# Causal attention inside a two-block kernel: one VectorE pass for mask, maximum and scaling, normalising on POOL, copies of the turned weights in turns

## The chip, the cores and the metric

The kernel runs on one core of a Trainium2 chip. The metric is the device time of one execution in microseconds. Before the change the median of three runs is 2840.65 us (2839.79 to 2842.64).

## What is computed

Two transformer blocks run one after the other over 1024 tokens of width 1024. The second block mixes tokens with an mLSTM and with multi-head attention, and the change lies in the attention. It has 8 heads. A query or key has 96 features (64 plain, 32 rotated), a value 64.

```python
def causal_block_attention(q, k, v):
    scale = dq ** -0.5
    def one_block(args):                     # 128 queries against all keys
        qblk, bi = args
        sc = jnp.einsum('bhqd,bkhd->bhqk', qblk, kf) * scale
        sc = jnp.where(kpos[None, :] <= qpos[:, None], sc, -jnp.inf)
        p = jax.nn.softmax(sc, axis=-1)
        return jnp.einsum('bhqk,bkhd->bqhd', p, vf)
```

In the kernel the mLSTM follows the attention, and behind both comes the output projection with the weights `w_out_2`.

## The kernel before

The five engines run programs of their own, written out by hand, and meet at counting semaphores (`wait_ge`). Within an engine the order is that of the code. The attention is in `mla_pe`, `mla_dve`, `mla_act`, `mla_pool` and `mla_sp` (PE is TensorE, DVE is VectorE, ACT is ScalarE, POOL is GpSimd, SP issues loads).

The work is cut into 64 blocks, listed in `NQ` (L2185). A block is one head and 128 queries. The two heads of a pair alternate, and the block of queries grows from i = 0 to 7, so the rows of block n have N = 128 (i + 1) keys: two blocks of 128, two of 256, up to two of 1024, and this four times. Keys beyond the block of queries are not computed.

For each block n TensorE computes the scores into the PSUM tile `PS[n % 2]` (`scores`, L2367). VectorE adds the triangular mask `negm` to the last 128 columns in place (L2319), takes the maximum of each row (L2321) and multiplies it by minus the scale (L2323). ScalarE computes the exponentials from PSUM into the SBUF tile `x4[:, n % 2]`, and their sum (L2243). VectorE inverts the sum (L2310) and multiplies the row by it (`normalise`, L2312). TensorE transposes the row in pieces of 128x128 into `PS[2]` (`turn`, L2377). ScalarE copies it to one of four tiles `turned_p` in SBUF (`pt_copy`, L2268). For each pair of blocks TensorE multiplies the turned weights with the values into `PS[3]` (`values`, L2390), and every fourth pair a half row of results leaves (`mixa` on ScalarE L2278, `mixa_low` on VectorE L2283).

The orders: TensorE takes scores(n + 2), turn(n), and after each odd n the values of the pair before. VectorE takes mask, maximum and scaling of block n, then normalises block n - 1. ScalarE takes the exponentials of block n, then the copy of block n - 1. The scores of n + 2 wait until the exponentials of n are done. A turn waits until the copy of the block before it is done. In the last sixteen blocks ScalarE and VectorE also do first steps of the mLSTM between blocks (`head_hi` L2454, `head_lo` L2464, `mask_dve` L2540, `log_weight_act` L2546).

POOL splits fp32 weights into a high and a low part by two passes over tensors (L499, L503, `split_unit`; for the heads' weights L483, L485). During the attention it waits for the sixteenth result (`pv_ready`), and then splits two units of `w_out_2`, in pieces of 256 columns. `in2_pool` (L1936 on) is its part of the projection before the attention, with one small memset (L1944).

## Time and profile before

| | us |
|---|---|
| median of 3 runs | 2840.65 |
| the profiled execution | 2838.5 |
| its span | 2836.8 |
| TensorE busy | 2729.4 (96%) |
| VectorE busy | 1814.4 (64%) |
| POOL busy | 1277.9 (45%) |
| ScalarE busy | 1021.3 (36%) |

The profile is of one execution on the chip, and the attention lies between 1780 and 1953 us of its span. A line names the engine, the line of the kernel (L2312), the operation, and output and inputs as `out<-in`. Idle before is the time for which the engine stood still before an instruction, with what ended it. PEld is the loading of TensorE's stationary operand, which overlaps its products (PE). The granted clock is a share of TensorE's full speed.

### The profile page before, as it was taken

To read this page: it belongs to the slowest core of one execution; us is meant where nothing else is said; L and a number is where in the kernel's file an instruction comes from. 1 tells how busy PE (TensorE), PEld (TensorE's weight loads), DVE (VectorE), ACT (ScalarE), POOL (GpSimd) and SP (SyncE) were. 2 spreads that over 40 slices of the span, in tenths; PEclk is the share of its full clock that TensorE was granted. 3 is DMA by queue.
4 is the path that set the end of the run, shared out by engine and by line. 5 is a ranking of instruction groups with operands and counts; after the bars stand their busy time and mean duration, and the time that the engine had idled before them with its cause. 6 is when DMAs were issued, how large, how long until landed. Compare 5 with 4: busy or idle time off the path is not lost.

```text
span 2836.8 us, 32978 instructions
## 1 busy us (share of the span) xinstructions
PE 2729.4 (96%) x12578; PEld 2155.0 (76%) x12578; DVE 1814.4 (64%) x2070; ACT 1021.3 (36%) x1397; POOL 1277.9 (45%) x780
## 2 busy tenths in 40 slices
PE   7999999999999999999998999889998999999998
PEld 5888788787777888887786887555587788878777
DVE  3111355655747766669879758776637766777887
ACT  4000323332214333334444014665535433344444
POOL 2433322223436988884333444102332888833321
PEclk9999999999999999999999999999899999999999
DMA  5223232324442333336631534103333345565543
GB/s 180 96 95 108 88 119 90 119 90 156 148 141 79 100 112 102 90 118 215 205 115 49 187 112 117 33 33 97 102 127 104 119 141 163 173 206 163 163 134 134
DMA packets 336967, 348.90 MB, mean 123 GB/s; under 512 B 18915, under 2 KB 256602, under 8 KB 336822
## 3 DMA queue, kind: packets, MB, share of 16 engines
q1 hardware_dynamic: 327254, 311.30, 35.6%
q10 hardware_dynamic: 9568, 35.66, 3.2%
q8 instruction: 93, 1.52, 0.2%
q14 instruction: 52, 0.43, 0.0%
HBM read 237.53 MB, written 108.34 MB: 122 GB/s over the span
## 4 chain that ended last, share of the span: by engine, by line
PE 51%; DVE 10%; issue 2%; ACT 2%; DMA 1%; POOL 1%; SPq 0%; DVEq 0%; ACTq 0%; POOLq 0%
PE ps L3282 34%; PE ps L533 9%; DVE op_lo L3359 2%; PE ps L2367 1%; PE ps L2740 1%; DVE sw_lo L3192 1%; PE ps L2390 1%; DVE small L2321 1%; PE ps L2377 1%; DVE x L2312 1%; PE ps L2858 1%; DVE acc L3603 1%; DVE acc L3610 0%; PE ps L2713 0%; DVE acc L1889 0%
## 5 line engine op out<-in xcount | busy, mean ns | idle before, releaser
L3282 PE MATMUL ps<-op_hi,sw_hi 128*128 128x512 f32 x1769 | 692.6, 392 | 15.5 <-DVE op_lo L3359 8.2
L3282 PE MATMUL ps<-op_hi,sw_lo 128*128 128x512 f32 x1769 | 689.1, 390 | 0.0
L3282 PE MATMUL ps<-op_lo,sw_hi 128*128 128x512 f32 x1769 | 688.9, 389 | 0.0
L499 POOL TENSOR_TENSOR w_hi_t<-w_raw,ones 128x1024 fp32r<-128x1024 f32 (+1 forms) x85 | 162.1, 1910 | 735.7 <-PE ps L533 354.7
L3282 PEld LDWEIGHTS ps<-op_hi,sw_hi 128*128 128x128 f32 x1769 | 332.4, 188 | 96.8 <-issue 16.8
L3282 PEld LDWEIGHTS ps<-op_hi,sw_lo 128*128 128x128 f32 x1769 | 332.4, 188 | 69.2
L3282 PEld LDWEIGHTS ps<-op_lo,sw_hi 128*128 128x128 f32 x1769 | 332.6, 188 | 68.7 <-issue 0.5
L656 DVE TENSOR_TENSOR stage<-ps,rstd 128x1024 f32<-128x1024 f32 x62 | 75.8, 1222 | 345.4 <-PE ps L533 326.9
L3182 ACT ACTIVATE sw_hi<-sw_sumNone 128x512 fp32r<-128x512 f32 (+1 forms) x252 | 157.1, 624 | 330.3 <-PE ps L3282 247.0
L533 PE MATMUL ps<-h1hi,w_hi_t 128*128 128x512 f32 x720 | 233.5, 405 | 13.0 <-DVE h1lo L617 9.0
L3192 POOL TENSOR_TENSOR sw_lo<-sw_sumNone,sw_hi 128x512 fp32r<-128x512 f32 x138 | 214.7, 1565 | 33.2 <-ACT sw_hi L3182 33.1
L533 PE MATMUL ps<-h1lo,w_hi_t 128*128 128x512 f32 x720 | 227.4, 397 | 0.0
L533 PE MATMUL ps<-h1hi,w_lo_t 128*128 128x512 f32 x720 | 227.0, 396 | 0.0
L503 POOL TENSOR_TENSOR w_lo_t<-w_raw,w_hi_t 128x1024 fp32r<-128x1024 f32 (+1 forms) x85 | 217.6, 2563 | 6.2
L3143 POOL TENSOR_TENSOR sw_sumNone<-sw_raw 128x512 f32<-128x512 f32 (+1 forms) x63 | 113.4, 1800 | 232.4 <-DVE sw_lo L3192 209.5
L3182 ACT ACTIVATE sw_hi<-sw_raw 128x512 fp32r<-128x512 f32 (+1 forms) x189 | 117.4, 622 | 200.6 <-PE ps L3282 198.8
L3192 POOL TENSOR_TENSOR sw_lo<-sw_raw,sw_hi 128x512 fp32r<-128x512 f32 x109 | 159.7, 1466 | 53.7 <-ACT sw_hi L3182 53.7
L533 PEld LDWEIGHTS ps<-h1hi,w_hi_t 128*128 128x128 f32 x720 | 133.8, 189 | 52.3 <-issue 10.5
L533 PEld LDWEIGHTS ps<-h1lo,w_hi_t 128*128 128x128 f32 x720 | 135.8, 189 | 33.4
L533 PEld LDWEIGHTS ps<-h1hi,w_lo_t 128*128 128x128 f32 x720 | 135.8, 189 | 33.2
L3158 POOL TENSOR_TENSOR sw_sumNone<-sw_raw,sw_sumNone 128x512 f32<-128x512 f32 (+1 forms) x63 | 91.4, 1450 | 87.5 <-DVE sw_lo L3192 84.8
L3150 POOL TENSOR_TENSOR sw_sumNone<-sw_sumNone,sw_raw 128x512 f32<-128x512 f32 (+1 forms) x63 | 98.7, 1566 | 61.6 <-DVE sw_lo L3192 58.9
(444 smaller groups left out, 4877.2 us busy)
## 6 DMA issues: line engine op xcount, KB each, us to landing
op_raw<-hidden SPq DMA_DIRECT2D x42, 1024.0 KB, 8.6
w_raw<-in_w_in SPq DMA_DIRECT2D x60, 512.0 KB, 3.9
sw_raw<-in_w_ffn_in SPq DMA_DIRECT2D x44, 512.0 KB, 5.3
proj<-stage ACTq DMA_DIRECT2D x42, 512.0 KB, 2.6
hidden<-hidden_blocks SPq DMA_DIRECT2D x13, 1536.0 KB, 6.2
acc<-proj SPq DMA_DIRECT2D x36, 512.0 KB, 4.5
hidden<-hidden_blocks SPq DMA_DIRECT2D x14, 1280.0 KB, 5.0
sw_raw<-in_w_up SPq DMA_DIRECT2D x32, 512.0 KB, 8.3
```

Of the source, the lines that this page charges most:

```text
L499: ins = pool.tensor_tensor(whi[:, u.par, s], raw[:, u.par, s], ones[:, 0:1].to_broadcast([P, n]), ALU.mult)
L503: ins = pool.tensor_tensor(wlo[:, u.par, s], raw[:, u.par, s], whi[:, u.par, s].bitcast(F32), ALU.subtract)
L533: mm = pe.matmul(out[:, b * HALF:(b + 1) * HALF], w, x[:, k, b * HALF:(b + 1) * HALF], start=(begin and k == ks[0] and n == 0), stop=(end ...
L656: dve.tensor_tensor(stage[:, u.par, :], PS[u.par if pair is None else pair][:, :], rstd[:, :], ALU.mult).then_inc(S["unit_out"][u.par], 1)
L2312: dve.tensor_scalar(x4[:, n % 2, 0:N], x4[:, n % 2, 0:N], sm(n, 3), None, ALU.mult)\
L3143: pool.tensor_tensor(s1, a21, a22, ALU.add).then_inc(S["sw_sum"], 1)
L3150: pool.tensor_tensor(s2, s1, a11, ALU.subtract).then_inc(S["sw_sum"], 1)
L3158: pool.tensor_tensor(s2, a12, s2, ALU.subtract).then_inc(S["sw_sum"], 1)
L3182: act.activation(wshi[ring(m)][:, 0:n], weight_block(p, r), ACT.Copy).then_inc(S["sw_hi"], 1)
L3192: eng.tensor_tensor(wslo[ring(m)][:, 0:n], weight_block(p, r), wshi[ring(m)][:, 0:n].bitcast(F32), ALU.subtract).then_inc(S["sw_lo"], 1)
L3282: mm = pe.matmul(out, w, x[:, k, :], start=(k == 0 and i == 0 and r < 4), stop=(k == n - 1 and i == 2), skip_group_check=r >= 4)
L3359: dve.tensor_tensor(lo_of(first, r)[:, :, :], fresh_of(first, r)[:, :, :], hi_of(first, r)[:, :, :].bitcast(F32), ALU.subtract).then_inc(S ...
```

## The change

Constants: while the projection before the attention runs, POOL also makes `mask_row`, a row of 1024 columns that is zero but for the triangle in its last 128.

VectorE: mask, maximum and scaling become one instruction, `tensor_tensor_reduce`. It adds the scores (PSUM) and the end of `mask_row` (SBUF), multiplies by minus the scale, writes the row to `x4[:, n % 4]`, and writes each row's minimum. ScalarE's exponentials read this row, with scale -1, and write it in place. Four rows of `x4` are in use instead of two, and the turned weights get four tiles of their own. The scores of n + 2 wait for the fused pass of n instead of its exponentials.

POOL: it multiplies each row by its inverse sum (64 `tensor_scalar` with one scalar for each partition), and after each odd block from 17 to 47 it does one piece of 256 columns of the two splits of `w_out_2`, which no longer wait for `pv_ready`.

Copies of the turned weights: ScalarE does those of the odd blocks up to 61, VectorE those of the even blocks and the last. VectorE's order is now: fused pass of block n, reciprocal of block n - 1, and for even n the copy of block n - 2.

The places where the mLSTM's first steps (`turn_v`, `weight_scores`) waited for the exponentials now wait for the fused pass.

```diff
@@ -1942,6 +1943,11 @@
                 if j == 2:
                     pool.wait_ge(S["unit_done"], U_IN2 + 2)
                     pool.memset(cb[:, :, 0:3], 0.0).then_inc(S["ml_consts"], 1)
+                    pool.memset(mask_row[:, :], 0.0).then_inc(S["ml_consts"], 1)
+                    pool.wait_ge(S["ml_consts"], 2)
+                    last = mask_row[:, T - P:T]
+                    pool.affine_select(out=last, in_=last, compare_op=ALU.is_ge, fill=-BIG, base=0,
+                                       pattern=[[-1, P]], channel_multiplier=1).then_inc(S["ml_consts"], 1)
...
-        turned_p = [x4[:, 2, :], x4[:, 3, :]] + [at(f"p_turned{n}", [P, T], kb)[:, :] for n, kb in ((2, 107.5), (3, 111.5))]
+        turned_p = [at(f"p_turned{n}", [P, T], kb)[:, :] for n, kb in enumerate((75.03125, 107.5, 79.03125, 111.5))]
...
@@ -2205,7 +2211,28 @@
             for h in range(8):
                 for i in range(2):
                     split_head(pool, h, i)
-            pool.wait_ge(S["pv_ready"], 16)
+            for n, (h, i) in enumerate(NQ):
+                N = (i + 1) * P
+                pool.wait_ge(S["rs_inv"], n + 1)
+                pool.tensor_scalar(x4[:, n % 4, 0:N], x4[:, n % 4, 0:N], sm(n, 2), None, ALU.mult)\
+                    .then_inc(S["p_norm"], 1)
+                if 16 <= n < 48 and n % 2:
+                    wo2_piece(pool, (n - 16) // 2)
+
+        def wo2_piece(pool, p):
+            u, i = Step(U_WO2 + p // 8), p % 8
+            s = slice(i % 4 * 2 * P, i % 4 * 2 * P + 2 * P)
+            if i == 0:
+                pool.wait_ge(S["w_landed"][u.par], u.landed())
+                pool.wait_ge(S["unit_done"], u.times(1, -1))
+            if i == 4:
+                pool.wait_ge(S["w_hi"], u.times(1, 1))
+            if i < 4:
+                ins = pool.tensor_tensor(whi[:, u.par, s], raw[:, u.par, s], ones[:, 0:1].to_broadcast([P, 2 * P]), ALU.mult)
+            else:
+                ins = pool.tensor_tensor(wlo[:, u.par, s], raw[:, u.par, s], whi[:, u.par, s].bitcast(F32), ALU.subtract)
+            if i % 4 == 3:
+                ins.then_inc(S[("w_hi", "w_split")[i // 4]], 1)
...
-                act.wait_ge(S["s_stat"], 2 * n + 2)
-                if n >= 2:
-                    act.wait_ge(S["pt_ready"], n - 1)
-                act.activation(x4[:, n % 2, 0:N], PS[n % 2][:, 0:N], ACT.Exp, bias=sm(n, 1), scale=QK_SCALE,
-                               accum_out=sm(n, 2)).then_inc(S["p_ready"], 1)
-                if n:
+                act.wait_ge(S["s_stat"], n + 1)
+                act.activation(x4[:, n % 4, 0:N], x4[:, n % 4, 0:N], ACT.Exp, bias=sm(n, 0), scale=-1.0,
+                               accum_out=sm(n, 1)).then_inc(S["p_ready"], 1)
+                if n and n % 2 == 0:
                     pt_copy(act, n - 1)
                 if n % 16 == 11:
...
         def sm(n, what):
 
-            c = 40 + 5 * (n % 2) + what
+            c = 40 + 3 * (n % 4) + what
             return small[:, c:c + 1]
...
+        def pt_copy_dve(dve, n):
+
+            N = (NQ[n][1] + 1) * P
+            dve.wait_ge(S["pt_ready"], n + 1)
+            if n >= 4:
+                dve.wait_ge(S["pv_ready"], n - 3)
+            dve.tensor_copy(turned_p[n % 4][:, 0:N], PS[2][:, 0:N]).then_inc(S["pt_out"], 1)
...
@@ -2303,26 +2334,22 @@
...
-            def normalise(n):
-
-                N = (NQ[n][1] + 1) * P
-                dve.wait_ge(S["p_ready"], n + 1)
-                dve.reciprocal(sm(n, 3), sm(n, 2)).then_inc(S["rs_inv"], 1)
-                dve.wait_ge(S["rs_inv"], n + 1)
-                dve.tensor_scalar(x4[:, n % 2, 0:N], x4[:, n % 2, 0:N], sm(n, 3), None, ALU.mult)\
-                   .then_inc(S["p_norm"], 1)
-
+            dve.wait_ge(S["ml_consts"], 3)
+            dve.wait_ge(S["q_rope"], 8)
             for n, (h, i) in enumerate(NQ):
                 N = (i + 1) * P
                 dve.wait_ge(S["s_ready"], n + 1)
-                late = PS[n % 2][:, N - P:N]
-                dve.tensor_tensor(late, late, negm[:, :], ALU.add).then_inc(S["s_masked"], 1)
-                dve.wait_ge(*count("s_masked", n + 1))
-                dve.tensor_reduce(sm(n, 0), PS[n % 2][:, 0:N], AX.X, ALU.max).then_inc(S["s_stat"], 1)
-                dve.wait_ge(S["s_stat"], 2 * n + 1)
-                dve.tensor_scalar(sm(n, 1), sm(n, 0), -QK_SCALE, None, ALU.mult).then_inc(S["s_stat"], 1)
+                if n == 3:
+                    dve.wait_ge(S["vh_t"], 8)
+                if n >= 4:
+                    dve.wait_ge(S["pt_ready"], n - 3)
+                dve.tensor_tensor_reduce(x4[:, n % 4, 0:N], PS[n % 2][:, 0:N], mask_row[:, T - N:T], -QK_SCALE, BIG,
+                                         ALU.add, ALU.min, sm(n, 0)).then_inc(S["s_stat"], 1)
                 if n:
-                    normalise(n - 1)
+                    dve.wait_ge(S["p_ready"], n)
+                    dve.reciprocal(sm(n - 1, 2), sm(n - 1, 1)).then_inc(S["rs_inv"], 1)
+                if n >= 2 and n % 2 == 0:
+                    pt_copy_dve(dve, n - 2)
                 if n % 16 == 12:
...
-            normalise(63)
+            dve.wait_ge(S["p_ready"], 64)
+            dve.reciprocal(sm(63, 2), sm(63, 1)).then_inc(S["rs_inv"], 1)
+            pt_copy_dve(dve, 62)
+            pt_copy_dve(dve, 63)
...
@@ -2361,7 +2391,7 @@
...
                 if n >= 2:
-                    pe.wait_ge(S["p_ready"], n - 1)
+                    pe.wait_ge(S["s_stat"], n - 1)
...
-                    tr = pe.transpose(PS[2][:, j * P:(j + 1) * P], x4[:, n % 2, j * P:(j + 1) * P], ident[:, :])
+                    tr = pe.transpose(PS[2][:, j * P:(j + 1) * P], x4[:, n % 4, j * P:(j + 1) * P], ident[:, :])
...
@@ -3882,8 +3912,6 @@
             f1_pool(pool)
             in2_pool(pool)
             mla_pool(pool)
-            for j in range(2):
-                split_unit(pool, Step(U_WO2 + j), pieces=4)
             mlstm_pool(pool)
```

## Rows read from the trace of the kernel before

**Rows 1.** Busy time by stretch: engines with instruction counts, granted clock, DMA share, GB/s

```profile
1780.00:1953.00 173.00, 150.69 (x1070) 96.28 (x1070) 126.05 (x338) 106.73 (x214) 10.57 (x16) 0.97 0.06 20
```

**Rows 2.** Waits before turns, by quarter; us in total, times, longest

```profile
PE ps L2377 <- DVE x L2312: 1.5, 4, 0.5
...
PE ps L2377 <- DVE x L2312: 3.9, 7, 0.9
PE ps L2377 <- ACT p_turned L2268: 2.0, 2, 1.0
...
PE ps L2377 <- DVE x L2312: 3.3, 7, 0.9
PE ps L2377 <- ACT p_turned L2268: 1.0, 1, 1.0
...
PE ps L2377 <- DVE x L2312: 6.8, 8, 1.4
```

**Rows 3.** Timeline, second and third quarter: start us, us, what, idle before

```profile
1840.03 0.49 DVE L2312 TENSOR_SCALAR x<-x,small 128x512 f32<-128x512 f32 x1
...
1879.00 0.30 DVE L2319 TENSOR_TENSOR ps<-ps,negm 128x128 f32<-128x128 f32 x1 [0.79 <-PE ps L2367]
...
1879.34 0.82 DVE L2321 TENSOR_REDUCE small<-ps 128x1 f32<-128x640 f32 x1
...
1880.27 0.15 DVE L2310 RECIPROCAL small<-small 128x1 f32<-128x1 f32 x1
...
1880.46 0.49 DVE L2312 TENSOR_SCALAR x<-x,small 128x512 f32<-128x512 f32 x1
...
1881.00 0.65 PE L2377 MATMUL ps<-ident,x 128*128 128x128 f32 x4 [0.51 <-DVE x L2312]
```

**Rows 4.** Groups of the attention stage by shape: count, busy us, mean ns, idle before

```profile
L2321 DVE TENSOR_REDUCE small<-ps 128x1 f32<-128x1024 f32 x8 | 9.8, 1225 | 0.3
L2312 DVE TENSOR_SCALAR x<-x,small 128x1024 f32<-128x1024 f32 x8 | 6.0, 754 | 0.3
L2312 DVE TENSOR_SCALAR x<-x,small 128x128 f32<-128x128 f32 x8 | 2.3, 288 | 0.3
L2243 ACT ACTIVATION_READ_ACCUMULATOR x<-ps,small 128x1 f32 x64 | 12.6, 197 | 0.0
L2268 ACT ACTIVATE p_turned<-ps 128x1024 f32<-128x1024 f32 x8 | 8.2, 1025 | 6.8 <-PE ps L2377 6.8
```

**Rows 5.** Groups of POOL by shape, whole span

```profile
L499 POOL TENSOR_TENSOR w_hi_t<-w_raw,ones 128x1024 fp32r<-128x1024 f32 x77 | 157.3, 2043 | 675.8 <-PE ps L533 354.7 <-DMA w_raw<-in_w_in 267.9 <-DMA w_raw<-in_w_branch_gla 30.1
L499 POOL TENSOR_TENSOR w_hi_t<-w_raw,ones 128x256 fp32r<-128x256 f32 x8 | 4.8, 624 | 59.9 <-PE ps L2390 59.9
L483 POOL TENSOR_TENSOR w_hi_t<-w_raw,ones 128x128 fp32r<-128x128 f32 x8 | 4.2, 524 | 10.3 <-PE ps L533 10.3
L860 POOL MEMSET wup<- 32x1024 f32 x1 | 0.9, 941 | 0.0
L681 POOL TENSOR_SCALAR_AFFINE_SELECT ident<-ident 128x128 f32<-128x128 f32 x1 | 0.3, 293 | 0.2 <-POOL negm L679 0.2
```

**Rows 6.** Timeline: VectorE beside POOL's splits, and POOL behind the small memset

```profile
1831.37 0.53 DVE L2312 TENSOR_SCALAR x<-x,small 128x256 f32<-128x256 f32 x1
...
1577.53 1.89 POOL L499 TENSOR_TENSOR w_hi_t<-w_raw,ones 128x1024 fp32r<-128x1024 f32 x1 [5.64 <-PE ps L533]
```

**Rows 7.** Instructions on the tile bytok, 1960 to 2060: ns min/median/max, starts

```profile
L2612 DVE RECIPROCAL bytok<-bytok x3: 203/203/203, 1977.4 to 2037.9; 128x8 f32<-128x8 f32 x3
...
L2618 DVE SCALAR_TENSOR_TENSOR bytok<-ps,bytok x3: 166/167/167, 1979.1 to 2039.6; 128x8 f32<-128x8 f32 x3
L2621 DVE TENSOR_SCALAR bytok<-bytok x3: 1984/1992/1992, 1979.3 to 2039.8; 128x8 f32<-128x8 f32 x3
```

**Rows 8.** One of four such instructions of line 2464 in the last quarter

```profile
L2464 DVE SCALAR_TENSOR_TENSOR q_parts<-stage,q_parts x1: 1223/1223/1223, 1913.8 to 1913.8; 64x1024 fp32r<-64x1024 f32 x1
```

**Rows 9.** Busy time by stretch, columns as in rows 1: start of the attention

```profile
1788.00:1792.00 4.00, 4.00 (x13) 1.75 (x12) 2.94 (x10) 2.11 (x6) 0.00 (x0) 0.50 0.00 0
```

More of the change, by code:

```diff
@@ L246 @@
          "out_row": ("kdt_ready", 8), "x3_squared": ("g_step", 24), "x3_summed": ("conv_step", 16), "qk_high": ("yb_ready", 8),
-         "qk_low": ("yb_scaled", 8), "s_masked": ("o_sum", 8),
+         "qk_low": ("yb_scaled", 8),
          "x3_last_spilled": ("mv_loaded", 64)}
@@ L437, in two_block_kernel @@
         orow = at("out_rows", [P, 4, T], R0 + 80)
+        mask_row = at("mask_row", [P, T], R0 + 128)
         ylast = at("y_last", [P, 2, HALF], R0 + 16)
@@ L2227, in mla_act @@
                 if h == 7:
-                    act.activation(small[:, 44:45], ones[:, 0:1], ACT.Exp)
+                    act.activation(small[:, 52:53], ones[:, 0:1], ACT.Exp)
                 act.wait_ge(S["unit_done"], uk.times(1, 1))
@@ L2254, in mla_act @@
                     log_weight_act(act, n - 58)
-            pt_copy(act, 63)
         def sm(n, what):
-            c = 40 + 5 * (n % 2) + what
+            c = 40 + 3 * (n % 4) + what
             return small[:, c:c + 1]
@@ L2679, in turn_v @@
             if h == 0:
-                pe.wait_ge(S["p_ready"], 64)
+                pe.wait_ge(S["s_stat"], 64)
             if h == 1:
@@ L2691, in weight_scores @@
             if n == 0:
-                pe.wait_ge(S["p_ready"], 63)
+                pe.wait_ge(S["s_stat"], 63)
             if J == 0:
```

## The prediction

> **What bounds the kernel now.** I read the busy time by stretches first. The change works in the attention stage, from 1780 to 1953 us, plus 1.2 us of constants earlier. There TensorE is busy for 150.7 of 173 us, VectorE for 126, ScalarE for 107 and POOL for 10.6 [rows 1]. So TensorE is close to its own load, and the change can gain no more than TensorE's idle time.
>
> Next, who made TensorE wait, by quarters of the stage (16 of the 64 blocks each; the same multiply of one quarter and of the next starts at 1840.03 and 1880.46, so a steady quarter takes 40.4 us [rows 3]). The turns (transposes) waited for VectorE's normalising for 1.5, 3.9, 3.3 and 6.8 us, and for ScalarE's copy of the turned weights for 2.0 (two waits, one of them at the end of the first quarter) and 1.0 us [rows 2]. That is 18.5 us in all: the cap of any gain, 0.65% of the run.
>
> Then the timeline of one pair of blocks, for the chain behind such a wait [rows 3]. TensorE's order is scores(n+2), turn(n), scores(n+3), turn(n+1), values. When the scores of block n+2 are complete (1879.00) VectorE, in order, adds the mask, reduces five blocks of 128 columns (0.82), scales, inverts the sum of block n+1 (1880.27), multiplies its four-block row (1880.46, 0.49), and only then can TensorE turn it, at 1881.00 after 0.51 idle. So it isn't VectorE's load that binds but its order: the row to be turned stands behind the whole pass over a later block. The second turn of each pair shows it. With k the width of the row in blocks of 128, those waits are 0.89, 0.77, 0.24, 0.51, 0.39, 0.27 and 0 for k = 1 to 7 (the first turn at k = 3 waits 0.25 more). At k = 8 the turn waits 1.0 for ScalarE's copy, which makes 4.3 us for that quarter [rows 2]. They add up to the 3.3 us and 7 waits of the third quarter's row; the 0.51 is shown in rows 3, and the others are its like.
>
> **The change, part by part.**
>
> *The mask and scaling go from VectorE.* Mask to reduction is 0.34 (1879.00 to 1879.34), the scaling about 0.08 between the end of the reduction and the reciprocal [rows 3]. The fused pass reads scores from PSUM and a mask row from SBUF, and writes a full row. I give it the reduction's duration, 1225 ns at 1024 columns [rows 4], which makes 0.16 + 0.133k. It must also deliver a minimum. The nearest row for such a read-out is ScalarE's, 197 ns [rows 4]. No VectorE instruction of the trace does this, so the cost is 0 to 0.19 on each chain, and could lie a little below 0 if the fused pass overlaps better. I take 0.05, nearer to the reduction, which delivers its result at no visible extra.
>
> *The multiply goes from VectorE to POOL.* VectorE took 288 ns at 128 columns and 754 at 1024 [rows 4], or 0.22 + 0.066k. In rows 3 the new order would be: fused pass 1879.00 to 1879.82, reciprocal to 1880.00, 0.05 to reach POOL, the multiply M(4), 0.05 to reach TensorE, so the turn starts at 1880.10 + M(4) instead of 1881.00. For any width the turn moves by M(k) - 0.64 - 0.066k. POOL has no such instruction in the trace. Above it is bounded by POOL's two-operand pass against a broadcast column, 524 ns at 128 and 2043 at 1024: about 0.33 + 0.2k. Below by an affine select, which reads one tensor (293 ns at 128), and by the pace of a memset (941 ns for 1024 columns): 0.18 + 0.107k [rows 5]. The operation reads one tensor, so I take it near the lower end, 0.22 + 0.12k: M(4) = 0.70, M(8) = 1.18. With this the turn moves by -0.42 + 0.054k: -0.37, -0.31, -0.26, -0.20, -0.15, -0.10 for k = 1 to 6, in sum -1.4 us for a quarter. At k = 7 there is no wait to win back.
>
> The Trainium skill (GPSIMD Engine Reference, § 4.1 Engine selection) says that POOL is about half as fast as VectorE on two-input elementwise work but roughly at line rate with one input. With its 1.03 cycles an element at 1.2 GHz (§ 3.1, Elementwise) M(4) would be about 0.44 plus a dispatch, an estimate from that page; the sum would then lie at my lower end. The trace shows the first half of this rule (524 to 2043 ns above) and nothing of the second.
>
> *Even copies of the turned weights go to VectorE.* turn(n+1) needs the copy of block n, and VectorE now starts it only after the fused pass of n+2 and the reciprocal of n+1. In rows 3 this is 1880.00 + 0.69 + 0.05 = 1880.74 against 1881.00, a gain of 0.26 at most at k = 4. Over the widths this path caps the gain at -0.45 + 0.066(k - 1). With my M it binds nowhere, with the lowest M from k = 3 on (a quarter then gains 1.7). At k = 8, where ScalarE's copy was what the turn waited for [rows 2], VectorE needs 1.22 instead of ScalarE's 1.02 for 1024 columns [rows 4]: +0.2 a quarter. VectorE's load over a pair falls even so (three passes over PSUM and two short ones instead of two masks, two reductions, two multiplies and four short ones), and ScalarE loses half of its copies. Its exponentials now read SBUF; I cost that at nothing, since they end well before VectorE comes to the reciprocal behind its next pass.
>
> *More buffers; TensorE's wait for scores(n+2) goes to the fused pass.* This wait hardly counted before, so nothing is gained.
>
> *Weight pieces on POOL.* The two units that POOL split in the second quarter (16 instructions, 10.6 us [rows 1]) now run as 16 pieces behind the odd multiplies of the second and third quarters. Before, they slowed VectorE's multiply: at 1831.37 it took 0.53 for 256 columns [rows 6], and the second quarter has 0.6 us more wait behind VectorE than the third [rows 2]. That goes. In its place a piece of some 0.62 us [rows 5] delays the next multiply where the row is narrow, some 0.3 a quarter. Net nothing. The next user of those weights is the projection behind the next stage.
>
> *POOL against VectorE on SBUF.* In the next stage, beside POOL, tiny VectorE instructions with a PSUM input or a reciprocal take 167 and 203 ns, but a scaling from SBUF to SBUF of the same 8 columns 1992 [rows 7]. The new VectorE work is of the two unhindered kinds. The Trainium skill (SBUF — State Buffer, § Who interferes with whom) says the same, and adds that VectorE instructions with two SBUF inputs block POOL's reads. Here these are four passes of 1.22 us for the next stage's heads in the last quarter [rows 8], each of which could hold one multiply back, up to 0.5 a time.
>
> *Last quarter.* Its 6.8 us of wait are 3.5 above the third quarter's, because those four passes (and four small ones) stand in VectorE's queue at narrow rows, where VectorE is full. The change takes about 1 us of VectorE's work from each such pair; I count 1.5 of the 3.5, between 0 and 3.
>
> *Constants.* A memset (0.94) and a select (0.29) [rows 5] stand on POOL's queue ahead of a weight split. POOL finished that one 5.64 us before TensorE let it begin the next [rows 6], so 1.3 us are hidden. Otherwise they would cost TensorE 1.3 once.
>
> **The sum**, against the profiled run's 2838.5 us (span 2836.8, 1.7 around it; the median of the timed runs is 2.15 above). Three quarters by -1.4 + 0.2 = -1.2, the first by -0.3 (it waits little, since TensorE runs at half clock there): -3.9. Last quarter's queue -1.5. Read-out 28 times 0.05: +1.4. Total -4.0: 2834.5 on the profiled run, 2836.7 as a median. Lower end: -1.5 three times, -0.5, -3.0 and -0.6 (no piece in the way): -8.6, so 2832. Upper end with POOL at its dear bound: below.
>
> **Rivals.**
>
> 1. *POOL's multiply becomes what the turns wait for: slower.* It takes over when M(4) passes about 0.84 (at 0.70 the gain is 4.0, and 28 turns a stage follow it one for one); slower by 0.2% from M(4) = 1.05. At the broadcast rate [rows 5] M(4) = 1.13: 28 x 0.43 = +12, and the first turn at k = 8 waits too (M(8) = 1.93), 0.9 in each quarter; less in the first, so about -4 + 14 = +10: 2851. With a dear read-out on top, 2856. For it: POOL is slow in every row where it computes, and its multiply sits on the path alone, with no neighbour to hide it. Against: all those rows stream two operands. Chance 0.22.
>
> 2. *The fused pass is dearer than a reduction.* With 0.19 more on each chain [rows 4] the sum is -4 + 28 x 0.14 = 0: 2840.6, the change of order does nothing. Chance 0.10.
>
> 3. *The clock.* After TensorE's idle at the stage's start its granted clock is 0.50 (1.2 GHz) in 1788 to 1792 [rows 9]. A stretch of 5 us at 0.50 costs 2.5 us of work. If the shifted pattern brings or saves one or two of them, the time moves by 2.5 to 5 either way: 2832 to 2842. Nothing in the change touches the idle that comes first, so I put 0.13.
>
> **How the numbers follow.** Forecast with its own range 2832 to 2840.6: 0.55. A measurement of this kernel tells 0.2% (5.7 us) from nothing: faster is below 2835.0, slower above 2846.3. The forecast gives 0.27 faster and 0.28 same; rival 1 0.19 slower and 0.03 same; rival 2 0.10 same; rival 3 0.05, 0.04 and 0.04. Together 0.32, 0.45 and 0.23. The range 2832 to 2852 leaves out rival 1 with a dear read-out and the lower tail, somewhat under 0.2.
>
> **What would show it.** Right: POOL's multiply near 0.70 us at 512 columns; TensorE's wait before turns about 13 to 15 us instead of 18.5, now put down to POOL and to VectorE's copy; the fused pass at 1.2 to 1.3 us for 1024 columns; a steady quarter of 39.2 instead of 40.4 us. Wrong: multiplies of over 1 us at 512 columns, a second instruction after each fused pass, VectorE's reciprocal or copy stretched beside POOL, or a difference that lies outside 1780 to 1953.

## The result and the profile after

The changed kernel takes 2861.22 us (median of 4 runs, 2858.78 to 2865.64) against 2840.86 us for the kernel before (2839.79 to 2842.64): the ratio is 1.0072, 95% interval [1.0057, 1.0087]. It is slower by 20.4 us, and lies above the forecast range.

The profiled execution of the changed kernel is the longest of the four (2865.64 us, span 2863.9), so its span is 27.1 us above that of before. Nearly 7 of that are not in the medians: this execution lies 4.4 above its median, and that of before 2.4 below its own. From the first score matmul of the attention to the first product on the tile Wt it takes 198.5 us (1777.6 to 1976.1), before 174.9 (1779.8 to 1954.7). All the attention figures below are read in this way. They are 23.6 us apart; the rest is small and scattered: 2.2 us less before the stage, 2.5 more in the next one, 3.2 more behind that.

First the busy time of the whole attention stage, the view of [rows 1], each kernel over its own stage. The line of after:

```profile
1778.00:1976.00 198.00, 155.94 (x1079) 99.95 (x1078) 88.15 (x243) 87.53 (x181) 122.64 (x81) 0.95 0.06 19
```

and the same view of the kernel before, over its 175 us (rows 1 stop 2 us earlier):

```profile
1780.00:1955.00 175.00, 152.69 (x1081) 97.49 (x1080) 126.15 (x339) 107.33 (x215) 11.80 (x17) 0.97 0.07 22
```

VectorE fell from 126 to 88 us and ScalarE from 107 to 88, as the change means. POOL rose from 12 to 123. TensorE's work is the same (1079 instructions against 1081); its idle time went from 22.3 to 42.1 us, and its busy time rose by 3.2 at a granted clock of 0.95 instead of 0.97. So 20 of the 23 us are waiting and 3 are longer busy time, which goes with the clock. Behind the start, the stage of before has a granted clock of 1.00 throughout. The changed kernel has two stretches there at 0.50, or 1.2 GHz (the first row takes in its edges). Each goes with one of TensorE's two longest waits for POOL: the clock fell just behind the wait of 2.13 us that ended at 1825.45, and during that of 2.19 us that ended at 1932.95. First the turn behind the earlier wait, then the busy time of both stretches, columns as in [rows 1]:

```profile
1825.45 1.54 PE L2407 MATMUL ps<-ident,x 128*128 128x128 f32 x8 [2.13 <-POOL x L2217]
...
1825.60:1829.10 3.50, 3.50 (x28) 3.17 (x29) 0.00 (x0) 1.40 (x3) 0.37 (x1) 0.55 0.00 0
1932.00:1938.60 6.60, 5.65 (x18) 3.22 (x19) 2.18 (x9) 3.18 (x7) 3.67 (x3) 0.50 0.00 1
```

TensorE is busy for 9.15 us in them; at full clock the same work would take about 4.4 us less (3.50 by 0.45, 5.65 by 0.50).

The waits of that stage (engine, line waited for, us in total, times, longest), which answer to [rows 2]:

```profile
DVE x L2346 <- PE ps L2397: 92.3, 39, 5.9
POOL x L2217 <- DVE small L2350: 79.8, 37, 14.8
PEld ps L2407 <- POOL x L2217: 62.6, 44, 3.0
...
PE ps L2407 <- POOL x L2217: 39.7, 34, 2.2
```

Line 2407 is the turn, 2217 POOL's multiply, 2346 the fused pass, 2350 the reciprocal. TensorE waited for POOL 39.7 us; before, its waits ahead of turns were 18.5 us [rows 2]. VectorE, whose idle time before was 49 us (175 less 126), now waits 92.3 us for scores. POOL itself waits 79.8 us for the reciprocal, so it isn't loaded to the brim: it is late.

The groups by shape say why. They answer to [rows 4] and [rows 5] (count, busy us, mean ns, idle before):

```profile
L2217 POOL TENSOR_SCALAR x<-x,small 128x1024 f32<-128x1024 f32 x8 | 22.7, 2843 | 1.2 <-DVE small L2350 0.6 <-DVE small L2362 0.6
...
L2217 POOL TENSOR_SCALAR x<-x,small 128x512 f32<-128x512 f32 x8 | 12.5, 1562 | 9.3 <-DVE small L2350 9.3
...
L2350 DVE RECIPROCAL small<-small 128x1 f32<-128x1 f32 x63 | 10.0, 158 | 0.5 <-ACT x L2268 0.3
L2346 DVE CUSTOM_DVE_ANT_0 x<-ps,mask_row 128x1024 f32<-128x1024 f32 x8 | 9.8, 1225 | 16.3 <-PE ps L2397 16.3
...
L2299 DVE COPY p_turned<-ps 128x1024 f32<-128x1024 f32 x5 | 6.1, 1224 | 6.3 <-PE ps L2407 6.3
...
L2346 DVE DVE_READ_ACCUMULATOR2_ANT small<- 128x1 f32 x64 | 5.3, 83 | 0.0
...
L2217 POOL TENSOR_SCALAR x<-x,small 128x128 f32<-128x128 f32 x8 | 4.8, 602 | 25.5 <-DVE small L2350 25.5
```

POOL's multiply of one tensor takes 602 ns at 128 columns, 1562 at 512 and 2843 at 1024: 0.28 + 0.32k with k in blocks of 128. I had given it 0.22 + 0.12k. The fused pass has the reduction's 1225 ns, and VectorE's copy 1224.

Last the timeline of a pair of blocks in the third quarter, which answers to [rows 3] (start us, us, what, idle before):

```profile
1894.86 0.96 DVE L2346 CUSTOM_DVE_ANT_0 x<-ps,mask_row 128x768 f32<-128x768 f32 x1 [3.18 <-PE ps L2397]
...
1895.75 0.08 DVE L2346 DVE_READ_ACCUMULATOR2_ANT small<- 128x1 f32 x1
1895.75 0.16 DVE L2350 RECIPROCAL small<-small 128x1 f32<-128x1 f32 x1
1895.82 0.80 DVE L2299 COPY p_turned<-ps 128x640 f32<-128x640 f32 x1
...
1896.00 1.88 POOL L2217 TENSOR_SCALAR x<-x,small 128x640 f32<-128x640 f32 x1 [1.74 <-DVE small L2350]
...
1897.85 0.73 POOL L2233 TENSOR_TENSOR w_lo_t<-w_raw,w_hi_t 128x256 fp32r<-128x256 f32 x1
...
1897.94 0.76 PE L2407 MATMUL ps<-ident,x 128*128 128x128 f32 x5 [1.27 <-POOL x L2217]
1898.55 2.20 POOL L2217 TENSOR_SCALAR x<-x,small 128x768 f32<-128x768 f32 x1
```

The scores are there at 1894.86, and 1.14 us later POOL begins to multiply. It needs 1.88, and TensorE, which had nothing else to do, stood idle 1.27 us until 1897.94. The copy on VectorE was over at 1896.62 and isn't in the way.

A steady quarter (from one multiply of 512 columns at 1844.11 to the same one at 1890.26) takes 46.15 us instead of 40.4 [rows 3].

### The profile page after: what moved, and what is told of

Read it like the earlier page. It is cut to its first block, busy times and chain, and to the rows that moved or that the text cites. A ratio compares the mean times of both kernels' runs of the same rounds, so it can differ in the third digit from the quotient of the medians.

```text
span 2863.9 us, 32917 instructions
## 1 busy us (share of the span) xinstructions
PE 2736.2 (96%) x12578; PEld 2160.1 (75%) x12578; DVE 1778.4 (62%) x1975; ACT 1001.2 (35%) x1364; POOL 1392.3 (49%) x846
## 4 chain that ended last, share of the span: by engine, by line
PE 51%; DVE 8%; POOL 3%; issue 3%; ACT 2%; DMA 1%; SPq 0%; DVEq 0%; ACTq 0%; POOLq 0%
PE ps L3312 34%; PE ps L534 9%; POOL x L2217 2%; DVE op_lo L3389 2%; PE ps L2397 1%; PE ps L2770 1%; PE ps L2407 1%; DVE sw_lo L3222 1%; PE ps L2420 1%; DMA op_raw<-hidden 1%; PE ps L2888 1%; PE ps L2743 1%; DVE acc L3633 1%; DVE acc L1890 0%; PE ps L576 0%
## 5 line engine op out<-in xcount | busy, mean ns | idle before, releaser
L500 POOL TENSOR_TENSOR w_hi_t<-w_raw,ones 128x1024 fp32r<-128x1024 f32 x77 | 158.7, 2061 | 670.9 <-PE ps L534 352.7
L504 POOL TENSOR_TENSOR w_lo_t<-w_raw,w_hi_t 128x1024 fp32r<-128x1024 f32 x77 | 211.8, 2751 | 6.0
L2217 POOL TENSOR_SCALAR x<-x,small 128x128 f32<-128x128 f32 (+7 forms) x64 | 112.0, 1753 | 80.4 <-DVE small L2350 79.8
```

Of the source, the lines that this page charges most:

```text
L500: ins = pool.tensor_tensor(whi[:, u.par, s], raw[:, u.par, s], ones[:, 0:1].to_broadcast([P, n]), ALU.mult)
L504: ins = pool.tensor_tensor(wlo[:, u.par, s], raw[:, u.par, s], whi[:, u.par, s].bitcast(F32), ALU.subtract)
L2217: pool.tensor_scalar(x4[:, n % 4, 0:N], x4[:, n % 4, 0:N], sm(n, 2), None, ALU.mult)\
```

## The experiments

Theory T: the loss is the price of POOL's multiply, standing alone between the reciprocal and the turn (the prediction's rival 1, at a price that I had not thought possible); what else is changed costs little or gains. Against it: (A) the copies in turns, (B) the weight pieces on POOL, (C) POOL and VectorE in each other's way, (D) what is dear is that POOL reads the scalar from a tile, not the form of the instruction. Each ratio is to the kernel before, measured alongside (2840.55 to 2841.32 us). The attention's length is compared beside the time, because the next stage, whose code is the same everywhere, took between 95.7 and 103.0 us from kernel to kernel. It is longer where its granted clock is lower: 95.7 us at 0.89 (experiment 1), 100.2 at 0.83 (before), 103.0 at 0.78 (experiment 5). Line numbers are each kernel's own; line 2217 is always POOL's multiply.

**1. The multiply back on VectorE, copies in turns stay.** The two weight units are split as before, behind `pv_ready` and not in pieces between multiplies.

```diff
-                pool.tensor_scalar(x4[:, n % 4, 0:N], x4[:, n % 4, 0:N], sm(n, 2), None, ALU.mult)\
-                    .then_inc(S["p_norm"], 1)
...
+                    dve.wait_ge(S["rs_inv"], n)
+                    normalise(dve, n - 1)
                 if n >= 2 and n % 2 == 0:
                     pt_copy_dve(dve, n - 2)
```

> The changed kernel with the multiply back on VectorE (behind the reciprocal and ahead of the even copy), and the two w_out_2 splits back behind pv_ready; fused pass and copies in turns stay. Theory A (POOL's multiply, 0.28 + 0.32 us per 128 columns, is what the turns wait for): the 20 us go, TensorE's waits before turns fall from 39.7 us to about 20, the copies on VectorE now stand behind the multiply and cost some 2 us a quarter, so 2840 to 2848. Theory B (the loss is in the copies that VectorE makes in turns, whatever does the multiply): above 2852.

Measured: 2841.3 us, ratio 1.0006 [0.9996, 1.0016], attention 179.4 us. The loss of 20 us is gone. What is left is a new wait (its waits, columns as above):

```profile
PE ps L2410 <- DVE p_turned L2298: 23.0, 30, 1.4
```

Line 2298 is the even copy. VectorE does it behind the fused pass, the reciprocal and the multiply, and the next turn needs it. So the multiply's move is what made the loss (the pieces moved too, but experiment 4 shows them to be worth nothing), and this version doesn't show the gain of the fused pass.

**2. Another instruction for the same multiply on POOL:** the two-operand product, with the inverse sum broadcast along the row.

```diff
-                pool.tensor_scalar(x4[:, n % 4, 0:N], x4[:, n % 4, 0:N], sm(n, 2), None, ALU.mult)\
+                pool.tensor_tensor(x4[:, n % 4, 0:N], x4[:, n % 4, 0:N], sm(n, 2).to_broadcast([P, N]), ALU.mult)\
```

> The changed kernel, with POOL's multiply as a two-operand product with the inverse sum broadcast along the row, in place of the scalar form. Theory A: what counts is the multiply's duration. If it runs at the pace of the weight splits (0.33 + 0.2 us per 128 columns, 1.13 at 512) the time falls by 28 x 0.43, about 10 to 12 us, to 2850. Rival C (POOL is slowed by VectorE's use of the SBUF port, not by the form of its instruction): the row of 1024 columns stays near 2.8 us and the time near 2861.

Measured: 2841.49 us, ratio 1.0001 [0.9992, 1.0011], attention 179.9 us. Its groups by shape and its waits:

```profile
L2217 POOL TENSOR_TENSOR x<-x,small 128x1024 f32<-128x1024 f32 x8 | 15.1, 1893 | 4.7 <-DVE small L2350 3.8 <-DVE small L2362 0.7
...
L2217 POOL TENSOR_TENSOR x<-x,small 128x512 f32<-128x512 f32 x8 | 8.3, 1039 | 12.2 <-DVE small L2350 12.2
...
L2217 POOL TENSOR_TENSOR x<-x,small 128x128 f32<-128x128 f32 x8 | 3.2, 400 | 24.5 <-DVE small L2350 24.5
```

```profile
PE ps L2407 <- POOL x L2217: 23.4, 32, 2.1
```

The product that reads two operands is the faster one: 0.19 + 0.213k against 0.28 + 0.32k. Only this duration is changed, by 0.52 us at 512 columns, and TensorE's wait falls from 39.7 to 23.4. This is the most direct evidence for T: the same engine and the same order at another price. (Expected was 1.13 us at 512 columns and 2850 us; it came out at 1.04 and 8.5 us lower.)

**3. The same form with a constant in place of the inverse sum.** The weights are multiplied by 0.5 and so aren't normalised.

```diff
-                pool.tensor_scalar(x4[:, n % 4, 0:N], x4[:, n % 4, 0:N], sm(n, 2), None, ALU.mult)\
+                pool.tensor_scalar(x4[:, n % 4, 0:N], x4[:, n % 4, 0:N], 0.5, None, ALU.mult)\
```

> The changed kernel, with POOL multiplying by the constant 0.5 in place of the inverse sum, so the weights are not normalised; same form, same waits. If the scalar read per partition is what makes the form dear, the row of 1024 columns takes about 1.2 us and the time is 2837 to 2842. If the form itself is dear, 2.8 us and 2861 as before.

Measured: 2864.41 us, ratio 1.0085 [1.0068, 1.0102], attention 195.3 us, waits for POOL 36.5 us. Groups by shape:

```profile
L2217 POOL TENSOR_SCALAR x<-x 128x1024 f32<-128x1024 f32 x8 | 22.1, 2771 | 1.3 <-DVE small L2350 0.6 <-DVE small L2362 0.6
...
L2217 POOL TENSOR_SCALAR x<-x 128x128 f32<-128x128 f32 x8 | 4.2, 528 | 25.5 <-DVE small L2350 25.5
```

The operand read from the tile costs 0.07 us a time, at every width. The price is the form's own, so D falls.

**4. The weight pieces behind all multiplies.**

```diff
                     .then_inc(S["p_norm"], 1)
-                if 16 <= n < 48 and n % 2:
-                    wo2_piece(pool, (n - 16) // 2)
...
+            for j in range(2):
+                split_unit(pool, Step(U_WO2 + j), pieces=4)
```

> The changed kernel, with the w_out_2 splits behind all multiplies instead of in pieces between them. Theory A: each of the 16 pieces (0.61 and 0.73 us) delays the next multiply only where that multiply was ready, so at most 16 x 0.67 = 10.7 us and, since the wide rows leave POOL idle in between, rather 3 to 6: 2855 to 2858. If pieces hide: 2861. The splits then delay POOL's first sum of the next stage by up to 11 us, which could give it back.

Measured: 2863.35 us, ratio 1.0085 [1.0068, 1.0103], attention 199.7 us, waits for POOL 39.0. Nothing is won, so B falls. In the timeline above a piece does hold the next multiply (it ends at 1898.58, and the multiply is there from 1898.55), but the turn behind that one comes only at 1901.26, after two blocks' scores and values.

**5. The fused pass alone:** multiply on VectorE, all copies on ScalarE, splits behind `pv_ready`, as before. POOL's loop goes, as in experiment 1.

```diff
                 if n:
                     dve.wait_ge(S["p_ready"], n)
                     dve.reciprocal(sm(n - 1, 2), sm(n - 1, 1)).then_inc(S["rs_inv"], 1)
-                if n >= 2 and n % 2 == 0:
-                    pt_copy_dve(dve, n - 2)
+                    dve.wait_ge(S["rs_inv"], n)
+                    normalise(dve, n - 1)
...
-                if n and n % 2 == 0:
+                if n:
                     pt_copy(act, n - 1)
```

> Only the fused pass of the change: multiply on VectorE, all copies of turned weights on ScalarE, the w_out_2 splits behind pv_ready. Against the run with the copies in turns (2841.3) it undoes the copies alone. By the chain, each odd turn comes 0.42 earlier (mask and scaling gone) where it waited that long: some 2.2 us a quarter, 6 to 9 in all, 2832 to 2835, with waits of turns of about 9 to 11 us. Rival: the fused pass brings nothing, since its read-out (83 ns) or ScalarE's reading from SBUF takes it back: 2840 and waits of 18 us.

Measured: 2824.65 us (5 runs, 2822.21 to 2828.63), ratio 0.9944 [0.9931, 0.9958], attention 161.3 us. Its waits ahead of turns, against [rows 2]:

```profile
PE ps L2408 <- DVE x L2283: 6.2, 12, 1.3
PE ps L2408 <- ACT p_turned L2292: 2.9, 3, 1.0
```

One of the change's three parts, without the rest, gains 16 us, where 6 to 9 were expected. Line 2283 is the multiply. The even copies' cost shows against this kernel: with the multiply on VectorE the copies in turns cost 18.1 us of attention (experiment 1, 179.4 against 161.3).

**6. POOL's multiply cut short.** It does only the first 128 columns of each row; wider rows are normalised in part.

```diff
-                pool.tensor_scalar(x4[:, n % 4, 0:N], x4[:, n % 4, 0:N], sm(n, 2), None, ALU.mult)\
+                pool.tensor_scalar(x4[:, n % 4, 0:P], x4[:, n % 4, 0:P], sm(n, 2), None, ALU.mult)\
```

> The changed kernel, with POOL multiplying only the first 128 columns of each row, so wide rows are only partly normalised: every multiply takes 0.60 us. If the rest of the sum was right and only POOL's price wrong, a multiply that averages 0.60 gives what I forecast for 0.76 on average or a little less, 2834 to 2838. If POOL's extra hand-over or VectorE's copies cost more than I counted, it stays above 2840.

Measured: 2829.41 us, ratio 0.9963 [0.995, 0.9976], attention 164.5 us, waits for POOL 9.9 us (16) and for VectorE's copy 3.8 (4). Order, semaphores, copies and pieces are the changed kernel's; only the duration is 0.60 us at every width (0.64 in the mean, by the few that VectorE's passes stretch, see below). The time is 5 us below what was expected. The other parts together then cost 3.2 us of attention against the fused pass alone. So A falls as the cause of this loss: the even copy costs the 18 us only where the multiply stands ahead of it on VectorE.

**7. The multiply on POOL, all copies back on ScalarE.** It fills the fourth corner of the square.

```diff
-                if n and n % 2 == 0:
+                if n:
                     pt_copy(act, n - 1)
...
-                if n >= 2 and n % 2 == 0:
-                    pt_copy_dve(dve, n - 2)
```

> The changed kernel (fused pass, multiply on POOL in its one-operand form, pieces on POOL), but ScalarE copies every block, so that only the multiply has moved beside the kernel with the fused pass alone (2824.7 us, 161.3 us of attention). Theory A (POOL's price alone makes the loss: 1.56 us at 512 columns is in the way whoever copies): TensorE's waits for POOL 35 to 40 us, attention 194 to 198 us, 2856 to 2861 us. Theory B (the two moves need each other: the even copy on VectorE holds up the reciprocal from which POOL starts, and without it POOL has room): waits 15 to 25 us, attention 172 to 182 us, 2835 to 2845 us. I expect A, somewhat below the changed kernel.

Measured: 2866.97 us, ratio 1.0085 [1.0068, 1.0102], attention 199.7 us, and the wait is where it was:

```profile
PE ps L2404 <- POOL x L2217: 39.0, 36, 2.6
```

Attention in us, multiply on VectorE: 161.3 (copies on ScalarE), 179.4 (in turns). Multiply on POOL in this form: 199.7 and 198.5. The two costs don't add. A turn starts when the last of its inputs is there, and with POOL at 1.56 us that is never the copy: no wait for it is in the profile. Theory A of this run holds, though the time is 5.8 us above the changed kernel's and not somewhat below.

**8. The changed kernel with the scores three blocks ahead.** TensorE does the scores of block n+3 before it turns block n, instead of n+2, and each copy stands one block later. POOL's slow form and its pieces stay.

```diff
+            scores(2)
             ...
-                if n + 2 < 64:
-                    scores(n + 2)
+                if n + 3 < 64:
+                    scores(n + 3)
...
-                if n and n % 2 == 0:
-                    pt_copy(act, n - 1)
+                if n >= 3 and n % 2:
+                    pt_copy(act, n - 2)
...
-                if n >= 2 and n % 2 == 0:
-                    pt_copy_dve(dve, n - 2)
+                if n >= 3 and n % 2:
+                    pt_copy_dve(dve, n - 3)
```

> The changed kernel with its slow multiply on POOL, but TensorE does the scores three blocks ahead of the turn instead of two, and each copy of turned weights stands one block later. Theory A (latency: POOL has 49 per cent of load, and its multiply only stands too late in a chain of one block's depth): a turn now has half a pair more room, 1.5 to 2.5 us at middle widths, and the waits for POOL fall below 15 us, attention 162 to 170 us, 2826 to 2835 us. Theory B (throughput, or the ends of the rows: narrow rows follow each other so fast that POOL at 0.28 + 0.32k cannot keep up, however far ahead): waits stay above 28 us, attention over 185 us, 2848 us or more. I expect something nearer to A.

Measured: 2828.88 us, ratio 0.9957 [0.994, 0.9973], attention 164.8 us. Its waits, and a piece of its timeline at the same widths as above:

```profile
PE ps L2407 <- DVE p_turned L2299: 12.5, 12, 1.9
...
PE ps L2407 <- POOL x L2217: 0.5, 1, 0.5
```

```profile
1878.38 1.88 POOL L2217 TENSOR_SCALAR x<-x,small 128x640 f32<-128x640 f32 x1
...
1880.11 0.96 DVE L2346 CUSTOM_DVE_ANT_0 x<-ps,mask_row 128x768 f32<-128x768 f32 x1 [1.82 <-PE ps L2397]
...
1882.02 0.73 PE L2407 MATMUL ps<-ident,x 128*128 128x128 f32 x5
```

The multiply takes the same 1.88 us, but it ended at 1880.26, 1.8 us before the turn at 1882.02. The wait for POOL fell from 39.7 to 0.5, and 32 us came back at an unchanged duration of the multiply. POOL's load was never too high; its distance to the turn was too short. The 12.5 us behind VectorE's copy are what turns wait for now.

**9. Scores three ahead on the fused pass alone.** As experiment 5, with the order of experiment 8 and each copy on ScalarE one block later.

```diff
-                if n:
-                    pt_copy(act, n - 1)
+                if n >= 2:
+                    pt_copy(act, n - 2)
...
-                if n + 2 < 64:
-                    scores(n + 2)
+                if n + 3 < 64:
+                    scores(n + 3)
```

> The fused pass alone, with TensorE's scores three blocks ahead of the turns instead of two (the four rows of x4 and the early release of PSUM allow it), and ScalarE's copy one block later in its order. Theory: what is left of the waits before turns comes from a multiply that stands behind the pass over a later block whose scores have only just come; one block more of distance takes them away but at the narrow rows. Waits below 4 us, 2825 to 2831. Rival: the load of VectorE or ScalarE takes over as the bound: no faster than the run with the fused pass alone.

Measured: 2821.07 us (5 runs, 2817.72 to 2822.17), ratio 0.9929 [0.9916, 0.9943], attention 155.4 us. It beats both kernels, the changed one by 40 us. Turns wait 6.9 us for ScalarE's copy and not for the multiply any more. Against experiment 5 the intervals of the ratios overlap, though no run of one reaches the runs of the other (at most 2822.17, at least 2822.21); the 5.9 us of attention are read from one profile each.

**10. The same, with the multiply on POOL as the two-operand product** and the weight pieces between multiplies, as in the changed kernel.

```diff
-                    dve.wait_ge(S["rs_inv"], n)
-                    normalise(dve, n - 1)
...
+                pool.tensor_tensor(x4[:, n % 4, 0:N], x4[:, n % 4, 0:N], sm(n, 2).to_broadcast([P, N]), ALU.mult)\
+                    .then_inc(S["p_norm"], 1)
```

> Scores three blocks ahead, fused pass, all copies on ScalarE one block later, and the multiply on POOL as a two-operand product against the sum's inverse broadcast (1.04 us at 512 columns, 1.89 at 1024); the same order with the multiply on VectorE took 2821.1 us and 155.4 us of attention. Theory A (with enough distance POOL's price is hidden, and VectorE's freed time buys nothing, since TensorE is already at its own load): 2818 to 2824 us, waits under 9 us. Theory B (VectorE's order still costs the 7 us that are left, and the move takes it away): waits under 3 us, 2813 to 2818 us. Theory C (even so POOL is late at narrow rows): waits of 12 us or more behind POOL, 2826 us or more.

Measured: 2821.65 us, ratio 0.9927 [0.991, 0.9943], attention 156.6 us:

```profile
1778.00:1936.00 158.00, 148.37 (x1080) 100.98 (x1080) 71.69 (x212) 109.93 (x217) 84.10 (x80) 0.97 0.10 26
```

With enough distance it makes no difference who multiplies. VectorE has 72 us of work here in 158, and nothing comes of the time that it is spared: TensorE is busy 148 of 158 us, and what is left of its waits before turns is ScalarE's copy (6.7 us) and 0.7 for POOL. Theory A of this run.

**Theory C in the traces.** No kernel tests it alone; the changed kernel's timeline of the last quarter shows both cases. Of 64 multiplies 62 have the one duration of their width (0.60, 0.92, 1.24, 1.56, 1.88, 2.20, 2.52 and 2.84 us for k = 1 to 8). The other two stand beside VectorE's passes for the next stage's heads, which read two tensors from SBUF:

```profile
1930.58 1.20 DVE L2494 SCALAR_TENSOR_TENSOR k_low<-stage,m2hi 64x1024 fp32r<-64x1024 f32 x1
...
1930.76 3.35 POOL L2217 TENSOR_SCALAR x<-x,small 128x384 f32<-128x384 f32 x2 [1.92 <-DVE small L2350]
...
1932.95 0.90 PE L2407 MATMUL ps<-ident,x 128*128 128x128 f32 x3 [2.19 <-POOL x L2217]
```

The entry of 3.35 us holds two multiplies of 384 columns. The first took 2.13 where 1.24 is the rule, 0.89 more, while VectorE ran from 1930.58 to 1931.78. The first turn of this width then waited 2.19 us and the second not at all; in the third quarter it was 0 and 0.86. The other case is at 1943.36 (640 columns, 2.98 against 1.88). In experiment 4 the same two multiplies are the long ones (2.13 and 2.98). So C is real, but small: at most the 2 us of the two delays, out of 20. Beside passes from PSUM nothing is stretched, on either engine: the fused pass at 1024 columns has 1225 ns with POOL at work and 1224 without (experiment 5).

## Why the prediction was wrong, point by point

*What bounds the kernel* was read rightly. It isn't VectorE's load that binds but its order: experiment 5 takes two short steps out of it (and 26 us out of VectorE's work, 126 to 101) and gains 16 us, while experiment 10 takes another 32 us of work from VectorE (71.7 us against 103.6 in 1778 to 1936) and gains nothing over experiment 9. The cap of 18.5 us held on the waits, but not as a cap of any gain: the stage of experiment 9 is 19.5 us shorter with 6.9 us of waits before turns left. 11.6 of the 19.5 are waits before turns, 1.0 is other idle time, and 6.9 are less busy time of TensorE (145.7 of 155.4 us, against 152.6 of 174.9), at a clock of 0.98 instead of 0.97. That last part was in no term of mine.

*POOL's multiply* is the step that failed. The term was M(k) = 0.22 + 0.12k, with M(4) = 0.70, and bounds of 0.18 + 0.107k and 0.33 + 0.2k. It measured M(4) = 1.56 and M(8) = 2.84, outside even the upper bound (1.13 and 1.93). I had taken POOL's two-operand pass for the dear end and argued "The operation reads one tensor, so I take it near the lower end". The one row on this side was another operation at one width (the affine select, 293 ns against 524 for the product at 128 columns [rows 5]), and no row had a tensor times a scalar. The form with one tensor and a scalar is dearer than the product, by a factor of 1.5 (1562 against 1039 ns, experiment 2). The Trainium skill's rule (GPSIMD Engine Reference, § 4.1 Engine selection), roughly line rate for one input, is not what this kernel shows: 1562 ns at 512 columns, where the estimate from its § 3.1 (Elementwise) was 0.44 us plus a dispatch. The measurement decides. The prediction put the rule into a sentence of its own, but its choice "near the lower end" went the same way without a row.

*The move of the turn*, M(k) - 0.64 - 0.066k, was right; only M was not. With the measured durations (0.60 to 2.52 us, above) it gives -0.10, +0.15, +0.40, +0.66, +0.91, +1.17 and +1.42 for k = 1 to 7. Added to the waits of before that makes 0.79, 0.92, 0.64, 1.17, 1.30, 1.44 and 1.42. The third quarter of the changed kernel has 0.75, 0.88, 0.86, 1.14, 1.27, 1.40 and 1.53 ahead of the second turn of those pairs: 7.8 us against 7.7 worked out. Three of them in the timeline:

```profile
1877.92 0.33 PE L2407 MATMUL ps<-ident,x 128*128 128x128 f32 x1 [0.75 <-POOL x L2217]
...
1891.88 0.66 PE L2407 MATMUL ps<-ident,x 128*128 128x128 f32 x4 [1.14 <-POOL x L2217]
...
1904.99 0.87 PE L2407 MATMUL ps<-ident,x 128*128 128x128 f32 x6 [1.40 <-POOL x L2217]
```

With the two turns at k = 8 (0.65 and 1.50) the quarter waits 10.0 us, 5.7 above the 4.3 of before, and the steady quarter is longer by just that (46.15 against 40.4).

*The sum without the failed step* can be tested, and it holds. Experiment 6 has a multiply of 0.60 us, near the 0.76 that I forecast in the mean over the widths. It waits 13.7 us before turns (forecast 13 to 15), and a steady quarter takes 38.9 us (1861.60 to 1900.49, first turn to first turn; forecast 39.2). Yet its stage is 10.4 us shorter, and not some 4. Waits before turns are 4.8 of that. Another 1.0 is TensorE's wait for the exponentials ahead of its scores, which I put at nothing. The other 4.5 are less busy time, and about 2.7 of that go with the clock at the stage's start: 0.89 in its first 16 us, where before has 0.68 (12.86 by 0.32 against 12.41 by 0.11).

```profile
1779.80:1795.80 16.00, 12.86 (x45) 6.40 (x45) 10.88 (x37) 9.55 (x26) 0.00 (x0) 0.68 0.16 36
...
1780.50:1796.50 16.00, 12.41 (x59) 6.88 (x58) 8.04 (x32) 9.54 (x25) 4.21 (x7) 0.89 0.21 50
```

The first line is of before, the second of experiment 6. The rest of the 4.5 stays open.

*The fused pass.* Duration 1225 ns: as forecast. The read-out exists (83 ns), and the reciprocal starts beside it (both at 1895.75), so 0.05 was enough and rival 2 falls. Its gain was in the sum, inside the 0.64, but never stood alone: about 0.37 on each of 28 chains, some 10 us. Alone it took the waits from 18.5 to 9.1 us, and 13.6 us off the attention and 16 off the time. A sum of its own for each part would have shown that the fused pass carried the gain and that the multiply's move could only give it away.

*Even copies on VectorE.* "With my M it binds nowhere" is right for the changed kernel (no wait for it in the profile), by way of a POOL that is later still. Where the multiply is short (experiment 6) it binds at k = 8 alone, for 1.19 us in each of three quarters, which is the 1.0 + 0.2 of the prediction. The cost with the multiply ahead of it on VectorE, 18 us, was not in the prediction.

*Pieces*: net nothing, as said (experiment 4). *Constants*: nothing of them is in the profile's waits. *POOL against VectorE*: as said in kind (the Trainium skill, SBUF — State Buffer, § Who interferes with whom, names VectorE instructions with two SBUF inputs, and the trace agrees), but I had allowed up to 0.5 a time, and two of the four passes held a multiply up, by 0.89 and 1.09. *Last quarter*: counted by turns, its waits rose from 6.8 to 10.7 us, those of the third quarter from 4.3 to 10.0. The rise is 1.8 smaller, near the 1.5 that I counted as gain there, though the loss buries it.

*Rival 1* is what happened, by its mechanism and at the price that its own rule asks for: slower from M(4) = 1.05. At the measured 1.56, 28 chains by the 0.86 above 0.70 give +24 - 4 = +20. That it stands so close to the 20.4 us of the medians is partly luck: the attention grew by 23.6, of which waits before turns are 21.2 (18.5 to 39.7). At M(4) = 1.04 the same sum gives +5.5, and in experiment 2 the waits grew by 4.9 and the attention by 5.0, while the time grew by 0.2 (ratio 1.0001). The next stage was 1.8 shorter there, and the profiled execution of before lies 2.4 under its median; a difference of a few us in the time says less than one in the waits. From experiment 2 to the changed kernel 0.52 us at 512 columns cost 18.6 us of attention, 36 for each us and not 28: wider rows grow more (0.95 at 1024 columns), both turns at k = 8 wait, and the clock takes its part. *Rival 3* is there at its size, two more stretches at 0.50 and 3.2 us more busy time of TensorE in the stage, but not from where I looked. I argued that nothing touches the idle at the stage's start; both stretches go with waits of over 2 us that the change itself brought. It adds to the loss and doesn't decide it.

The range failed since both ends of M came from rows of other instructions, and being hemmed in by them was taken for a proof. A bound is one only if a reason excludes what lies beyond it.

What stays open: why a one-tensor multiply is slower than a two-tensor product on POOL, and why the next stage is granted another clock from kernel to kernel (0.78 to 0.89).

## What to carry to other kernels

Where work moves to an engine whose instruction of that form the trace doesn't show, write down the price from which the change turns into a loss, and measure that one instruction first; here 1.05 us at 512 columns was the point, and the form taken cost 1.56 while another form of the same multiply cost 1.04. If a slow engine sits alone between two steps of TensorE, look at its distance before its load: one more block of scores ahead hid 1.56 us (0.5 us of waits for POOL were left) and turned +20 us into -12. And give each part of a change its own sum: one part (the fused pass) carried the whole gain, and a later part spent it.

## What the runs showed of the hardware

- POOL, fp32 in SBUF, 128 partitions: tensor times a scalar per partition takes 602, 1562 and 2843 ns at 128, 512 and 1024 columns; with a constant 528, 1488 and 2771; the product with a column broadcast 400, 1039 and 1893.
- VectorE's fused add, scale and minimum from PSUM with a row written to SBUF takes 1225 ns at 1024 columns, as long as the plain reduction did [rows 4], and its result is read out by a second instruction of 83 ns, beside which the next one begins.
- A pass of VectorE over two SBUF tensors (1.20 us) held a multiply on POOL up by 0.89 us, another by 1.09; beside passes from PSUM 62 of 64 multiplies kept one duration for each width.
- The same multiply on VectorE takes 754 ns at 1024 columns [rows 4], so POOL is slower by a factor of 3.8 in one form and 2.5 in the other.
- Just behind a wait of TensorE of 2.13 us, and during one of 2.19 us, its granted clock fell to 0.50, for some 3.5 and 6.6 us; the rest of the stage, behind its start, had 1.00.
